# Reordered closing sums of a one-layer decoder kernel, with the norm weights multiplied on GpSimd

## The chip, the cores and the metric

The kernel runs on one core of one Trainium2 chip. The metric is the device time of one execution in microseconds; runs of the kernel before and of the changed kernel are compared by their medians. The engines are named as the profile names them: PE is TensorE, DVE is VectorE, ACT is ScalarE, POOL is GpSimd and SP is SyncE, which only issues transfers here.

## The reference, cut to what matters

One layer of a decoder on 512 tokens of 1024 float32 features: a mixing sub-layer (sparse attention and retention), then a mixture of experts. Only the very end of the second sub-layer is touched here:

```python
def _rms_norm(x, g=None):
    y = xf * lax.rsqrt(jnp.mean(xf * xf, axis=-1, keepdims=True) + EPS)
    return y * g
...
    for e in range(N_EXPERTS):          # 32 experts, each token uses 2 of them
        hid = silu(t @ w_gate_exp[e]) * (t @ w_up_exp[e])
        y = y + combine[:, e:e + 1] * (hid @ w_down_exp[e])
...
    h_res = h_res + gate2 * _rms_norm(ffn, g_post_ffn)
```

So the output is the residual plus a row-normalised sum of two expert rows for each token, times one weight vector (`gate2 * g_post_ffn`, kept in the kernel as `G2`).

## The kernel before

The experts are worked through in units of up to 128 (token, expert) pairs. All units but the last write their weighted rows to `pair_rows` in device memory, two rows for each token (indirect DMAs of GpSimd). The last unit is not written: its 128 rows stay in SBUF (`YO`), and TensorE brings them to their tokens with a product by a 0/1 matrix (`SEL`).

After the last scatter SyncE reads `pair_rows` back in `NB` = 4 blocks of 128 tokens: `YG[b][:, 0, :]` is a token's first row and `YG[b][:, 1, :]` its second (blocks 0 and 1 in the tile `rows`, blocks 2 and 3 in `both_bufs`); semaphore `y_back[b]` tells that block b is there. Then, for each block:

- TensorE (`collect`, L1153 to L1164) writes the 0/1 product to PSUM, two matmuls of 512 columns, each seen in the trace as two records. For blocks 0 and 1 that is all, and DVE adds the two rows of a token itself (`both_rows`, L1957). For blocks 2 and 3 TensorE also adds the second rows, by a product with the identity (L1163), for which it waits on `y_back[b]`.
- DVE adds PSUM to the first rows (`combine`, L1963). This gives the block's sum.
- ACT sums the squares and takes the root (L1407, L1409), DVE inverts it (`invert`, L1967).
- DVE multiplies by `G2` and by the inverse root. For blocks 0 and 1 that is one instruction (`scale`, L1975). For block 2 DVE multiplies by `G2` (`weigh`, L1971) and ACT by the inverse root (L1412). For block 3 DVE does both, and adds the residual in the last step (L1995, in two halves).
- Blocks 0 to 2 go out as accumulating DMAs that GpSimd issues (L2104): the residual already lies in `out`, and the DMA adds to it. Block 3 goes out as two plain halves that SyncE issues (L748).

The order on each engine is the order in which the code is written. A `link` on DVE makes its next instruction wait until the linked one has completed. `y_sum` counts finished sums, `y_scaled` blocks that are ready to go out, and `sel_done` blocks that TensorE has finished.

Of the kernel before, what the change touches and what calls it, by code (L numbers as in the profile page):

```python
# [21 lines left out]
P = 128  # L22
D = 1024
S = 512
NB = S // P
# [237 lines left out]
def build(nc, t, out):  # L263
# [3 lines left out]
    with ExitStack() as ctx:  # L267
# [3 lines left out]
        def sem(name):  # L271
            return ctx.enter_context(nc.semaphore(name))
# [139 lines left out]
        y_sq, o_add = sem("y_sq"), sem("o_add")  # L412
        x2_out, y_inv, y_scaled = sem("x2_out"), sem("y_inv"), sem("y_scaled")
        y_back = [sem(f"y_back{b}") for b in range(NB)]
# [108 lines left out]
        SEL = [score[:, i * S:(i + 1) * S] for i in range(DIRECT)]  # L523
        SUM_BANK, SUMMED = (2, 4, 0, 6), 2

# [230 lines left out]
        def _(pe):  # L756
# [397 lines left out]
            def collect(u, b):  # L1154
                for n in range(2):
                    if b == 0:
                        pe.wait_ge((y_evA, y_evV)[n], NU)
                    c = slice(n * 512, (n + 1) * 512)
                    mm = pe.matmul(ps[SUM_BANK[b] + n][:, :], SEL[u - NS][:, b * P:(b + 1) * P], YO[u % 2][:, c],
                                   start=True, stop=(b < SUMMED))  # L1160
                    if b >= SUMMED:
                        pe.wait_ge(y_back[b], 16)
                        mm = pe.matmul(ps[SUM_BANK[b] + n][:, :], ident, YG[b][:, 1, c], start=False, stop=True)  # L1163
                mm.then_inc(sel_done, 1)  # L1164
# [16 lines left out]
            for b in range(NB):  # L1181
                collect(NS, b)


        @block.scalar
        def _(act):
# [218 lines left out]
            for b in range(NB):  # L1405
                act.wait_ge(y_sum, b + 1)
                a.activation(JUNK2, YG[b][:, 0, :], ACT.Square, accum_out=yss[:, b:b + 1]).then_inc(squared, 1)  # L1407
                act.wait_ge(squared, 2 * NB + b + 1)
                a.activation(yr[:, b:b + 1], yss[:, b:b + 1], ACT.Sqrt, bias=eps, scale=1.0 / D).then_inc(y_sq, 1)  # L1409
                if b == NB - 2:  # L1410
                    act.wait_ge(y_inv, b + 1)
                    a.activation(YG[b][:, 1, :], YG[b][:, 1, :], ACT.Identity, bias=zero,  # L1412
                                 scale=yss[:, b:b + 1]).then_inc(y_scaled, 1)


        @block.vector
        def _(dve):
# [3 lines left out]
            def link(ins):  # L1421

                chained[0] += 1
                ins.then_inc(v_chain, 1)
                dve.wait_ge(v_chain, chained[0])
# [539 lines left out]
            def invert(b):  # L1965
                dve.wait_ge(y_sq, b + 1)
                relay(v.reciprocal(yss[:, b:b + 1], yr[:, b:b + 1]), y_inv, b + 1)  # L1967

            def weigh(b):
                y = YG[b]  # L1970
                link(v.tensor_tensor(y[:, 1, :], y[:, 0, :], G2, ALU.mult))  # L1971

            def scale(b):
                y = YG[b]
                v.scalar_tensor_tensor(out=y[:, 1, :], in0=y[:, 0, :], scalar=yss[:, b:b + 1], in1=G2, op0=ALU.mult,  # L1975
                                       op1=ALU.mult).then_inc(y_scaled, 1)

# [3 lines left out]
            combine(1)  # L1981
            invert(0)
            scale(0)
            combine(2)
            weigh(2)
            invert(1)
            scale(1)
            invert(2)
            combine(3)
            weigh(3)  # L1990
            invert(3)
# [8 lines left out]
        def _(pool):  # L2000
# [98 lines left out]
            each_overflow(pool, lambda: pool.wait_ge(xt_mm, 2 * NU), overflow)  # L2099
            pool.sem_inc(y_base, 1)  # L2100
            pool.wait_ge(x2_out, 16 * NB)
            for b in range(NB - 1):
# [24 lines left out]
```

## Time and profile before

| | us |
|---|---|
| median of 3 runs | 684.8 |
| lowest and highest run | 684.11, 686.64 |
| span of the profiled execution, first to last instruction | 686.0 |

The profiled execution is one more execution. Its own record is the span of 686.0 us, no separate time outside the span is given for it, and the span lies within the three runs. A sum against the trace is therefore a difference against 686.0, and that difference is then put on the median of 684.8.

TensorE is busy for 633.2 us of the span (92%) and DVE for 375.3 us (55%). The stretch that the change touches is the last 23 us, from about 663 us, after the last unit's down projection. In that stretch the shares of the whole span say nothing, and the timeline and the chain of waits are read instead.

### The profile page before, as it was taken

How to read it: one execution, taken by the hardware profiler on the slowest of the kernel's cores; microseconds unless marked ns; L12 is line 12 of the kernel's file. 1: busy time of each engine (PE TensorE's matmuls, PEld its weight loads, DVE VectorE, ACT ScalarE, POOL GpSimd, SP SyncE). 2: the span in 40 equal slices, each digit the busy share in tenths (PEclk: the TensorE clock that was granted, in tenths of full speed). 3: DMA queues.
4: the chain of work that ended last, by engine and by line, in shares of the span. 5: the costliest groups of instructions: out<-in, count | busy, mean ns of one | idle time of the engine just before them, and what ended most of it. 6: DMA issues, size and time to landing. Idle time of an engine off the chain costs nothing.

```text
span 686.0 us, 7088 instructions
## 1 busy us (share of the span) xinstructions
PE 633.2 (92%) x2400; PEld 298.5 (44%) x2400; DVE 375.3 (55%) x721; ACT 206.1 (30%) x411; POOL 100.3 (15%) x96
## 2 busy tenths in 40 slices
PE   1599999999999999999989999989999999988883
PEld 1364444444344444546644556433434453433331
DVE  5765667999786773246863336862323333232055
ACT  1453443334254544431121322111212121221023
POOL 1004333300122221000000000112121211110101
PEclk9999999999999999999989997999999999998998
DMA  9992715240606144070396129799999999999997
GB/s 329 394 374 96 277 28 216 59 187 7 240 0 204 43 147 162 13 241 31 125 383 289 61 86 402 269 370 409 419 421 419 420 419 420 419 418 413 409 411 157
DMA packets 52757, 174.70 MB, mean 255 GB/s; under 512 B 9712, under 2 KB 9712, under 8 KB 41840
## 3 DMA queue, kind: packets, MB, share of 16 engines
q1 hardware_dynamic: 45136, 160.26, 60.3%
q0 software_dynamic: 6160, 12.10, 5.5%
q10 hardware_dynamic: 1424, 1.87, 0.8%
q8 instruction: 20, 0.33, 0.2%
q14 instruction: 17, 0.14, 0.1%
HBM read 168.43 MB, written 15.21 MB: 268 GB/s over the span
## 4 chain that ended last, share of the span: by engine, by line
PE 73%; DVE 11%; DMA 7%; issue 4%; SPq 2%; ACT 1%; POOLq 0%; DVEq 0%; ACTq 0%
PE psum L772 16%; PE psum L1052 15%; PE psum L1113 8%; PE psum L775 8%; PE psum L920 7%; DMA both_bufs<-pair_rows 3%; DMA ring<-in_w_ada 2%; DVE score L1536 2%; PE psum L1025 2%; DVE sm L1535 2%; DVE score L1766 2%; SPq L647 2%; DVE rows L1459 2%; PE psum L877 2%; PE psum L897 1%
## 5 line engine op out<-in xcount | busy, mean ns | idle before, releaser
L772 PE MATMUL psum<-hT,ring 128*128 128x512 f32 (+1 forms) x320 | 135.8, 579 | 0.0
L1052 PE MATMUL psum<-ring,hT 128*64 128x512 f32 (+2 forms) x320 | 92.2, 594 | 1.8 <-DMA ring<-in_w_up_exp 1.4
L772 PEld LDWEIGHTS psum<-hT,ring 128*128 128x128 f32 x320 | 60.2, 192 | 69.4 <-issue 60.1
L775 PE MATMUL psum<-ring,hT 128*128 128x512 f32 x192 | 85.2, 597 | 0.0
L1885 DVE TENSOR_SCALAR work<-work 128x256 f32<-128x256 f32 x16 | 4.6, 290 | 101.8 <-PE psum L1062 76.0
L1248 ACT ACTIVATE both_bufs<-psum 32x512 f32<-32x512 f32 (+2 forms) x68 | 38.3, 563 | 67.7 <-PE psum L772 66.7
L1459 DVE SCALAR_TENSOR_TENSOR rows<-ring,sm,rows 128x512 f32<-128x512 f32 x64 | 55.5, 866 | 1.7
L775 PEld LDWEIGHTS psum<-ring,hT 128*128 128x128 f32 x192 | 35.6, 190 | 44.6 <-issue 44.2
L1052 PEld LDWEIGHTS psum<-ring,hT 128*64 128x64 f32 (+2 forms) x320 | 31.7, 142 | 48.8 <-issue 46.3
L1347 ACT ACTIVATE work<-psum 128x256 f32<-128x256 f32 x17 | 6.5, 383 | 146.7 <-PE psum L1052 146.7
L1113 PE MATMUL psum<-ring,work 128*64 128x512 f32 (+1 forms) x160 | 40.1, 598 | 0.7 <-ACT work L1353 0.7
L2059 POOL DMA_INDIRECT pair_rows<-work,pid_t x16 | 16.0, 1000 | 152.9 <-DVE work L1897 152.9
L1052 PE MATMUL psum<-both_bufs,hT 128*64 128x512 f32 x64 | 31.1, 643 | 3.4 <-issue 3.4
L1052 PE MATMUL psum<-xs,hT 128*64 128x512 f32 x64 | 31.2, 644 | 0.0
L920 PE MATMUL psum<-ring,hT 128*128 128x512 f32 x64 | 30.4, 623 | 0.7 <-ACT hT L1222 0.7
L920 PE MATMUL psum<-ring,work 128*128 128x512 f32 x64 | 28.7, 593 | 0.9 <-ACT work L1301 0.9
L2012 POOL TENSOR_TENSOR both_bufs<-both_bufs 128x512 f32<-128x512 f32 (+1 forms) x13 | 15.5, 1191 | 94.9 <-ACT both_bufs L1248 94.9
L795 PE MATMUL psum<-cst,work 128*64 128x1 f32 x64 | 8.3, 259 | 22.7 <-DVE work L1459 22.7
L1897 DVE TENSOR_SCALAR work<-psum,sinT 128x512 f32<-128x512 f32 x17 | 12.8, 751 | 29.9 <-PE psum L1113 25.4
L1887 DVE RECIPROCAL work<-work 128x256 f32<-128x256 f32 x16 | 28.0, 1753 | 0.5
L1052 PE MATMUL psum<-rows,hT 128*64 128x512 f32 x64 | 28.2, 593 | 0.0
L1535 DVE MAX8 sm<-score 128x8 f32<-128x256 f32 (+2 forms) x48 | 26.7, 556 | 1.2
(322 smaller groups left out, 912.9 us busy)
## 6 DMA issues: line engine op xcount, KB each, us to landing
ring<-in_w_down_exp SPq DMA_DIRECT2D x20, 1024.0 KB, 18.4
ring<-in_w_in SPq DMA_DIRECT2D x8, 2048.0 KB, 9.3
ring<-in_w_ada SPq DMA_DIRECT2D x8, 2048.0 KB, 13.8
ring<-in_w_gate_exp SPq DMA_DIRECT2D x14, 1024.0 KB, 20.2
ring<-in_w_up_exp SPq DMA_DIRECT2D x14, 1024.0 KB, 23.0
ring<-in_w_ada SPq DMA_DIRECT2D x7, 1024.0 KB, 13.3
ring<-in_w_gate_exp SPq DMA_DIRECT2D x12, 512.0 KB, 15.2
ring<-in_w_up_exp SPq DMA_DIRECT2D x12, 512.0 KB, 15.4
```

What stands on the lines that cost most here:

```text
L647: sp.dma_start(chunk(n)[:, lo:hi, :], w_ada[:, lo:hi, what * 512:(what + 1) * 512]).then_inc(signal, 16)
L772: mm = pe.matmul(o[:, at], w[:, k, b * P:(b + 1) * P], hT3[:, k, at], start=(k == 0), stop=(k == KD - 1))
L775: mm = pe.matmul(o[:, :], hT3[:, k, b * P:(b + 1) * P], w[:, k, :], start=(k == 0), stop=(k == KD - 1))
L920: mm = pe.matmul(o[:, :], mixed, w[:, k, :], start=(k == 0), stop=(k == KD - 1))
L1052: mm = pe.matmul(o[rows, :], XT[u % 2][:, k, rows], both(GU_SLOT[place])[:, k, :, :], start=(k == 0), stop=(k == KD - 1))
L1113: mm = pe.matmul(o[rows, :], HT[u % 2][:, i, rows], down_of(DOWN_SLOT[place])[:, i, n * 512:(n + 1) * 512], start=(i == 0), stop=(i == KF ...
L1248: ins = a.activation(SWAPPED[r % 2][here, at], bank(s)[there, at], ACT.Copy)
L1459: ins = v.scalar_tensor_tensor(out=acc, in0=w[:, k, :], scalar=sc_[:, k:k + 1], in1=acc, op0=ALU.mult, op1=ALU.add)
L1535: link(v.max(top8, m))
L1887: v.reciprocal(e, e).then_inc(gu_step, 1)
L2012: g.tensor_tensor(other, other, trig[table][:, 1, at], ALU.mult).then_inc(crossed, 1)
L2059: g.indirect_dma_start(out=y_dram, out_offset=bass.IndirectOffsetOnAxis(ap=pid_t[:, u:u + 1], axis=0), in_=YO[u % 2], in_offset=None, boun ...
```

## The change

- TensorE does the 0/1 products of all four blocks first, without waiting for a transfer, and signals each block as its product is ready. It adds second rows for block 3 alone, behind all products (`add_last_rows`). Block 2's rows are now added by DVE (`both_rows(2)`).
- GpSimd multiplies the sums of blocks 0, 1 and 2 by `G2`. Its DMA issues stand behind all three multiplications in its program.
- DVE's `scale` is now a multiplication by the inverse root alone (one tensor and one scalar of each partition), and waits for GpSimd's product.
- ACT no longer scales block 2.
- DVE's order is new: the sums of blocks 2 and 3 stand ahead of the scaling of block 1.

```diff
@@ TensorE
                 for n in range(2):
                     if b == 0:
                         pe.wait_ge((y_evA, y_evV)[n], NU)
-                    c = slice(n * 512, (n + 1) * 512)
-                    mm = pe.matmul(ps[SUM_BANK[b] + n][:, :], SEL[u - NS][:, b * P:(b + 1) * P], YO[u % 2][:, c],
-                                   start=True, stop=(b < SUMMED))
-                    if b >= SUMMED:
-                        pe.wait_ge(y_back[b], 16)
-                        mm = pe.matmul(ps[SUM_BANK[b] + n][:, :], ident, YG[b][:, 1, c], start=False, stop=True)
+                    mm = pe.matmul(ps[SUM_BANK[b] + n][:, :], SEL[u - NS][:, b * P:(b + 1) * P],
+                                   YO[u % 2][:, n * 512:(n + 1) * 512], start=True, stop=(b < NB - 1))
+                if b < NB - 1:
+                    mm.then_inc(sel_done, 1)
+
+            def add_last_rows():
+
+                b = NB - 1
+                pe.wait_ge(y_back[b], 16)
+                for n in range(2):
+                    mm = pe.matmul(ps[SUM_BANK[b] + n][:, :], ident, YG[b][:, 1, n * 512:(n + 1) * 512], start=False,
+                                   stop=True)
                 mm.then_inc(sel_done, 1)
@@ ScalarE
                 a.activation(yr[:, b:b + 1], yss[:, b:b + 1], ACT.Sqrt, bias=eps, scale=1.0 / D).then_inc(y_sq, 1)
-                if b == NB - 2:
-                    act.wait_ge(y_inv, b + 1)
-                    a.activation(YG[b][:, 1, :], YG[b][:, 1, :], ACT.Identity, bias=zero,
-                                 scale=yss[:, b:b + 1]).then_inc(y_scaled, 1)
@@ VectorE
-            def weigh(b):
-                y = YG[b]
-                link(v.tensor_tensor(y[:, 1, :], y[:, 0, :], G2, ALU.mult))
-
             def scale(b):
                 y = YG[b]
-                v.scalar_tensor_tensor(out=y[:, 1, :], in0=y[:, 0, :], scalar=yss[:, b:b + 1], in1=G2, op0=ALU.mult,
-                                       op1=ALU.mult).then_inc(y_scaled, 1)
+                dve.wait_ge(y_weighed, b + 1)
+                v.tensor_scalar(y[:, 1, :], y[:, 1, :], yss[:, b:b + 1], None, ALU.mult).then_inc(y_scaled, 1)
 
             both_rows(0)
             combine(0)
             both_rows(1)
             combine(1)
             invert(0)
+            both_rows(2)
             scale(0)
             combine(2)
-            weigh(2)
             invert(1)
+            combine(3)
             scale(1)
+            link(v.tensor_tensor(YG[3][:, 1, :], YG[3][:, 0, :], G2, ALU.mult))
             invert(2)
-            combine(3)
-            weigh(3)
+            scale(2)
             invert(3)
@@ GpSimd
             pool.sem_inc(y_base, 1)
+            for b in range(NB - 1):
+                pool.wait_ge(y_sum, b + 1)
+                g.tensor_tensor(YG[b][:, 1, :], YG[b][:, 0, :], G2, ALU.mult).then_inc(y_weighed, 1)
             pool.wait_ge(x2_out, 16 * NB)
             for b in range(NB - 1):
                 pool.wait_ge(y_scaled, b + 1)
```

The order on DVE before, from the second `both_rows` (L1957) to the last reciprocal (`rows` holds blocks 0 and 1, `both_bufs` blocks 2 and 3, `work` in an operand is `G2`):

```order
L1957 TENSOR_TENSOR rows<-rows 128x1024 [waits y_back1,y_sum]
L1963 TENSOR_TENSOR rows<-rows,psum 128x1024 [waits sel_done,v_chain]
L1967 RECIPROCAL sm<-sm 128x1 [waits y_sq,y_sum]
L1975 SCALAR_TENSOR_TENSOR rows<-rows,sm,work 128x1024 [waits y_inv]
L1963 TENSOR_TENSOR both_bufs<-both_bufs,psum 128x1024 [waits sel_done]
L1971 TENSOR_TENSOR both_bufs<-both_bufs,work 128x1024 [waits y_sum]
L1967 RECIPROCAL sm<-sm 128x1 [waits y_sq,v_chain]
L1975 SCALAR_TENSOR_TENSOR rows<-rows,sm,work 128x1024 [waits y_inv]
L1967 RECIPROCAL sm<-sm 128x1 [waits y_sq]
L1963 TENSOR_TENSOR both_bufs<-both_bufs,psum 128x1024 [waits sel_done,y_inv]
L1971 TENSOR_TENSOR both_bufs<-both_bufs,work 128x1024 [waits y_sum]
L1967 RECIPROCAL sm<-sm 128x1 [waits y_sq,v_chain]
```

Each sum of blocks 2 and 3 is followed directly by its product with `G2`. The same stretch of DVE after the change, from the first reciprocal on:

```order
L1970 RECIPROCAL sm<-sm 128x1 [waits y_sq,y_sum]
L1960 TENSOR_TENSOR both_bufs<-both_bufs 128x1024 [waits y_back2,y_inv]
L1975 TENSOR_SCALAR rows<-rows,sm 128x1024 [waits y_weighed,v_chain]
L1966 TENSOR_TENSOR both_bufs<-both_bufs,psum 128x1024 [waits sel_done]
L1970 RECIPROCAL sm<-sm 128x1 [waits y_sq,y_sum]
L1966 TENSOR_TENSOR both_bufs<-both_bufs,psum 128x1024 [waits sel_done,y_inv]
L1975 TENSOR_SCALAR rows<-rows,sm 128x1024 [waits y_weighed,y_sum]
L1988 TENSOR_TENSOR both_bufs<-both_bufs,work 128x1024
L1970 RECIPROCAL sm<-sm 128x1 [waits y_sq,v_chain]
L1975 TENSOR_SCALAR both_bufs<-both_bufs,sm 128x1024 [waits y_weighed,y_inv]
L1970 RECIPROCAL sm<-sm 128x1 [waits y_sq]
```

The second-row sum of block 2 (L1960) has come in ahead of the first scaling, and the first scaling waits both for it (`v_chain`) and for GpSimd (`y_weighed`). On GpSimd, the end of the program, the difference of after against before:

```order
-L2104 DMA out<-rows 128x1024 [waits y_scaled,x2_out]
-L2104 DMA out<-rows 128x1024 [waits y_scaled]
-L2104 DMA out<-both_bufs 128x1024 [waits y_scaled]
+L2103 TENSOR_TENSOR rows<-rows,work 128x1024 [waits y_sum] x2
+L2103 TENSOR_TENSOR both_bufs<-both_bufs,work 128x1024 [waits y_sum]
+L2107 DMA out<-rows 128x1024 [waits y_scaled,x2_out]
+L2107 DMA out<-rows 128x1024 [waits y_scaled]
+L2107 DMA out<-both_bufs 128x1024 [waits y_scaled]
```

The three issues of the accumulating DMAs have moved behind three multiplications, the last of which waits for the third sum.

## Rows read from the trace of the kernel before

**Rows 1.** Chain that ended last, in order of time: start us, us, what.

```profile
649.90 18.68 DMA both_bufs<-pair_rows
...
668.62 1.12 PE psum L1163 x2
...
675.61 1.24 ACT both_bufs L1412
...
678.64 0.75 DVE both_bufs L1995
```

**Rows 2.** Timeline: start us, us, engine, line, operation, out<-in, shape, count, idle before.

```profile
663.32 4.53 PE L1159 MATMUL psum<-work,score 128*128 128x512 f32 x10
...
666.63 1.23 DVE L1957 TENSOR_TENSOR rows<-rows 128x1024 f32<-128x1024 f32 x1
...
667.89 1.22 DVE L1963 TENSOR_TENSOR rows<-rows,psum 128x1024 f32<-128x1024 f32 x1
...
669.35 1.28 DVE L1975 SCALAR_TENSOR_TENSOR rows<-rows,sm,work 128x1024 f32<-128x1024 f32 x1
...
671.23 0.99 POOL L2104 DMA_DIRECT2D out<-rows  x1 [30.00 <-DVE rows L1975]
...
675.80 0.89 POOL L2104 DMA_DIRECT2D out<-rows  x1 [3.59 <-DVE rows L1975]
...
677.14 0.84 POOL L2104 DMA_DIRECT2D out<-both_bufs  x1 [0.45 <-ACT both_bufs L1412]
...
679.42 1.23 SPq L748 DMA_DIRECT2D out<-both_bufs  x2
```

**Rows 3.** Windows: stretch, length, busy of each engine, PEclk, DMA share, GB/s.

```profile
672.40:676.00 3.60, 2.50 (x6) 0.76 (x4) 3.46 (x6) 1.84 (x4) 0.20 (x1) 1.00 0.90 146
676.00:677.20 1.20, 0.00 (x0) 0.00 (x0) 1.17 (x2) 1.19 (x2) 0.75 (x2) 1.00 0.01 0
677.20:680.40 3.20, 0.00 (x0) 0.00 (x0) 2.46 (x4) 1.11 (x3) 0.78 (x1) 0.87 1.11 170
680.40:683.20 2.80, 0.00 (x0) 0.00 (x0) 0.00 (x0) 0.00 (x0) 0.00 (x0) 0.50 0.97 195
683.20:684.80 1.60, 0.00 (x0) 0.00 (x0) 0.00 (x0) 0.00 (x0) 0.00 (x0) 0.50 0.79 302
```

**Rows 4.** Instructions of the tile `pair_rows` from 600 us on, transfer times.

```profile
DMA to landing us min/median/max: 6.7/11.8/20.7
```

**Rows 5.** Timeline: POOL's products of two float32 SBUF tensors, early in the kernel.

```profile
64.78 1.00 POOL L2012 TENSOR_TENSOR both_bufs<-both_bufs 128x384 f32<-128x384 f32 x1 [2.76 <-ACT both_bufs L1248]
...
94.04 1.27 POOL L2012 TENSOR_TENSOR both_bufs<-both_bufs 128x512 f32<-128x512 f32 x1 [5.08 <-ACT both_bufs L1248]
```

**Rows 6.** Timeline: three places where DVE and POOL work at once.

```profile
79.48 1.34 POOL L2012 TENSOR_TENSOR both_bufs<-both_bufs 128x512 f32<-128x512 f32 x1 [3.89 <-ACT both_bufs L1248]
79.73 1.37 DVE L1481 TENSOR_SCALAR xs<-xs 128x512 f32<-128x512 f32 x1
...
86.29 0.69 DVE L1521 TENSOR_TENSOR work<-psum,both_bufs 128x512 f32<-128x512 f32 x1 [2.03 <-ACT both_bufs L1248]
86.35 1.27 POOL L2012 TENSOR_TENSOR both_bufs<-both_bufs 128x512 f32<-128x512 f32 x1 [2.63 <-ACT both_bufs L1248]
86.90 0.86 DVE L1764 TENSOR_SCALAR score<-both_bufs,sm 128x256 f32<-128x256 f32 x1
...
196.41 3.21 DVE L1459 SCALAR_TENSOR_TENSOR rows<-ring,sm,rows 128x512 f32<-128x512 f32 x3
196.53 1.75 POOL L2015 TENSOR_TENSOR ring<-ring,both_bufs 128x512 f32<-128x512 f32 x1
```

**Rows 7.** Groups by line and shape: count, busy us, mean ns, idle before.

```profile
L1481 DVE TENSOR_SCALAR both_bufs<-both_bufs 128x512 f32<-128x512 f32 x1 | 0.4, 426 | 0.0
...
L1764 DVE TENSOR_SCALAR score<-both_bufs,sm 128x512 f32<-128x512 f32 x1 | 0.5, 486 | 0.0
L1764 DVE TENSOR_SCALAR score<-both_bufs,sm 128x384 f32<-128x384 f32 x1 | 0.4, 408 | 0.0
```

More of the change, by code:

```diff
@@ L412, in build @@
         y_sq, o_add = sem("y_sq"), sem("o_add")
-        x2_out, y_inv, y_scaled = sem("x2_out"), sem("y_inv"), sem("y_scaled")
+        x2_out, y_inv, y_scaled, y_weighed = sem("x2_out"), sem("y_inv"), sem("y_scaled"), sem("y_weighed")
         y_back = [sem(f"y_back{b}") for b in range(NB)]
@@ L523, in build @@
         SEL = [score[:, i * S:(i + 1) * S] for i in range(DIRECT)]
-        SUM_BANK, SUMMED = (2, 4, 0, 6), 2
+        SUM_BANK = (2, 4, 0, 6)
         def load_gate(sp, e, s, signal):
@@ L1182, in _ @@
                 collect(NS, b)
+            add_last_rows()
         @block.scalar
```

## The prediction

> **What bounds the kernel now.** The change touches only the end, so I read the chain that ended last first, then the timeline from 663 us, then the windows of the DMA engines there. The chain [rows 1] shows that the end hangs on the read-back of block 2: that transfer lands at 668.58, TensorE adds its second rows from 668.62, DVE and ACT finish blocks 2 and 3, and DVE's last two halves start at 678.64. SyncE issues the last two transfers at 679.42 [rows 2].
>
> What the chain does not show is how full the DMA engines are behind that. GpSimd issues the accumulating transfers of blocks 0, 1 and 2 at 671.23, 675.80 and 677.14 [rows 2]. The first has the engines to itself: from 672.40 to 676.00 they move 3.6 x 146 = 526 KB, one block, at a share of 0.90. Then they idle (676.00 to 677.20, share 0.01). From 677.20 to 683.20 the share is about 1 and 3.2 x 170 + 2.8 x 195 = 1090 KB pass, which is blocks 1 and 2. The last block follows until 684.80 (1.6 x 302 = 483 KB), and the span ends at 686.0 [rows 3]. So a block by an accumulating transfer costs the engines 2.8 to 3.6 us, a plain one some 1.4 us, and from 677.2 to the end this is a queue that never runs dry. Block 0's transfer is out of that queue only because it starts 4.6 us earlier than the second. **The end is a matter of when the accumulating transfers can start, as much as of the last sum.**
>
> **The change part by part.**
>
> TensorE. The eight 0/1 products need 16 records. Ten took 4.53 us from 663.32 [rows 2], so at 0.43 each all 16 end at about 670.3. Block 3's second rows come with the slowest read-back: issued at about 650.4, landing after 20.7 us [rows 4], at 671.1. Two more matmuls (four records, 1.8 us) make block 3's product ready at about 672.9, where before DVE could begin that sum only at 675.61. Taken alone this is a gain of up to 2.7 us. Block 2 needs no matmul after its landing any more.
>
> GpSimd, the price of one multiplication. Its products of two SBUF tensors take 1.00 us for 384 columns and 1.27 for 512 [rows 5], so 0.27 for each 128 more, and 2.36 us for 1024 columns (an estimate along that line). Two instructions of 512 columns would take 2.54, which bounds it from above, and DVE's 1.23 for such a pair of tensors [rows 2] from below; the line through the two rows of the same operation is nearest. DVE did block 0's whole scaling in 1.28 us [rows 2].
>
> DVE and GpSimd at the same time. This is the term that decides. At 79.48 GpSimd starts a product of 1.34 us and DVE a one-tensor multiplication at 79.73 [rows 6], which alone takes 0.426 [rows 7]. It takes 1.37 and ends at 81.10, 0.28 after GpSimd's end at 80.82: it waited for the whole of GpSimd's instruction. With the scalar taken from SBUF, which is the form of the new `scale`, it is the same: 0.86 us for 256 columns at 86.90, ending 0.14 after GpSimd [rows 6], where 0.33 would be expected from 0.408 and 0.486 for 384 and 512 columns [rows 7]. DVE's addition that reads PSUM, at 86.29 beside the same GpSimd product, took its plain 0.69. The other way round, at 196.41 DVE starts the first of three additions of two SBUF tensors, and GpSimd's product at 196.53 takes 1.75 instead of 1.27, while DVE's three take 3.21 together [rows 6], about 1.0 more than three of the 0.75 that L1995, of the same kind and size, takes [rows 1]: GpSimd waited for DVE's first, and DVE's second for all of GpSimd. It follows that `both_rows`, the new `scale` and DVE's product with `G2` take turns with GpSimd's multiplications in whole instructions, and `combine` (which reads PSUM) does not. At a handover about 0.15 us is saved.
>
> The Trainium skill (SBUF — State Buffer, section SBUF: two separate sides) calls this an exclusive lock on a port pair, held for the full instruction, and names two-input and fast-mode DVE instructions; by it the term would be the same, and the trace agrees with 1.37 us against 0.43.
>
> Now the walk. Until 667.86 nothing moves: `both_rows(1)` starts at 666.63, as soon as the first sum is done and before GpSimd can, and ends at 667.86 [rows 2].
> - GpSimd's block 0: 667.86 + 2.36 - 0.15 = 670.1. Beside it DVE does `combine(1)` and the reciprocal.
> - `both_rows(2)` (data there since 668.58) waits, then 670.1 + 1.23 - 0.15 = 671.2.
> - GpSimd's block 1 is ready since 669.1. DVE's next instruction waits for `both_rows(2)` to complete (`v_chain`), and into that gap GpSimd steps, as it did at 197: 671.2 + 2.2 = 673.4.
> - `scale(0)` is held until then. Its own price is 0.486 + 4 x 0.078 = 0.80 [rows 7], so it ends at 674.0.
> - `combine(2)` stands behind it on DVE: 674.05 to 675.3. Before, it ended at 672.7.
> - GpSimd's block 2 waits for that: 675.4 to 677.8. DVE's reciprocal and `combine(3)` pass beside it, until 676.7, but `scale(1)` waits for 677.8 and ends at 678.4.
> - The product of block 3 with `G2` ends at 679.7, the reciprocal at 679.9, `scale(2)` at 680.7, the last reciprocal at 680.9. The last halves start at 680.9, and SyncE issues at about 681.7 and 682.4.
>
> TensorE's gain is thus not used: block 3's product waits from 672.9 to 675.5 for DVE. ACT's removed 1.24 us [rows 1] is no loss and no gain, since its squares are ready long before.
>
> GpSimd's DMA issues stand behind its third multiplication: the first goes out at 677.85 instead of 671.23, although block 0 is scaled at 674.0. The second follows at about 678.8 and the third at about 681.1. From issue to data it was 1.2 us for the first before (671.23 to 672.4), so the engines start at 679.05. They have three accumulating blocks and one plain one: 6.0 for two of them as before, 2.7 to 3.5 for the third, 1.4 for the last block, and 1.4 from the last data to the end of the span (684.6 to 686.0). 679.05 + 6.0 + 2.7 + 1.4 + 1.4 = 690.55, which is **4.6 us over 686.0**; with 3.5 it is 5.4. If all three flow at 2.7, it is 3.9. I take 4.6, since the third comes out of a queue that is already running, as the second of before did. The DVE side alone would end later by 681.7 - 679.4 = 2.3 us, so the queue of transfers decides.
>
> Put on the median: 684.8 + 4.6 = 689.4.
>
> **The rivals.**
>
> GpSimd does not get its turn between `both_rows(2)` and `scale(0)`. Against it speaks the wait for completion between the two; for it, that no row shows a DVE instruction this short behind. Then `scale(0)` ends at 672.0, `combine(2)` at 673.3, GpSimd's multiplications at 674.4 and 676.8, and all is 1.0 us earlier: +3.6, 688.4.
>
> The instructions do not hinder each other at this size. Then `combine(2)` ends at 672.5, the third multiplication at 675.0, and the first transfer is issued at 675.1. The queue of three still costs: 675.1 + 1.2 + 8.7 + 2.8 = 687.8 to 688.6, so +1.8 to +2.6, 686.6 to 687.4. Rows 6 speak against it.
>
> Not slower: the accumulating transfers are bound by their own latency and run side by side when all three wait at once. It decides if, with three queued, the bytes per us rise clearly over 195 GB/s. With hardly any hindrance on DVE, the last halves start at 677.1, 1.5 us before 678.64, and the result is 683.3. Against it: two transfers already overlapped in 677.2 to 683.2, and the rate was 170 to 195, not twice 146 [rows 3].
>
> Worse: the DMA descriptors of GpSimd are held up as its arithmetic is. `scale(1)` runs from 677.8 as the first issue starts, which would add up to 0.65 us; with the dear third transfer, 4.6 + 0.8 + 0.65 = +6.1, 690.9. The product with `G2` at 676.86 did not lengthen the issue at 677.14 (0.84 against 0.99 and 0.89) [rows 2].
>
> For this last point the Trainium skill (SBUF — State Buffer, the box on DVE blocking DMA) says that a fast-mode DVE instruction keeps GpSimd from writing descriptors. No run here shows it with `scale`'s form.
>
> **How the numbers follow.** The forecast 0.56, GpSimd's missed turn 0.14, no hindrance 0.16, transfers side by side 0.06, worse 0.08. Half a per cent is about what a measurement of this kernel can tell from no change, 3.4 us, so the border is 688.2. The forecast and the worse case lie above it almost wholly (0.54 and 0.07), of the missed turn a little over half (0.08): slower 0.69. The rest is same, 0.28, with 0.03 left for faster. The range goes from the lower end of no hindrance, 686.6, to the worse case, 691.0, and leaves out the side-by-side case and some of the worse.
>
> **What would show it.** In the profile after: GpSimd's three multiplications at about 667.9, 671.2 and 675.4 and each 2.2 to 2.5 us of own work; `scale(0)` ending right after the second of them, with 2.2 us of waiting inside it; `combine(2)` ending near 675.3; GpSimd's first DMA at 677.9; a DMA share near 1 without a hole from 679 to 689; the idle hole of before at 676.00 to 677.20 grown to the whole stretch from about 672.5 to 679. The prediction is wrong if `scale(0)` and `both_rows(2)` take 0.8 and 1.2 us beside GpSimd's work, or if three queued transfers take clearly less than 8 us.

## The result, and the profile after

The changed kernel takes 690.77 us in the median of four runs (689.47 to 692.2), against 685.07 us of four runs of the kernel before (684.11 to 686.64). The ratio is 1.0086, with a 95% interval of 1.0062 to 1.0110. It is slower by 5.7 us; forecast were 4.6 us and 689.4 us, in a range of 686.6 to 691.0 us. Among the runs further below, one execution of 1653.61 us (the kernel before with block 1 scaled early) is left out of the ratio.

The profiled execution of after has a span of 687.6 us, only 1.6 more than the 686.0 of before. That is no contradiction: the stretch ahead of the change differs from execution to execution by several us (TensorE's first 0/1 product starts at 663.32 in before and at 659.71 in after). All that the change does comes behind that product, so two profiles are compared here mainly by the **tail**: from the start of the first 0/1 product to the end of the span. It is 686.0 - 663.32 = 22.7 us before and 687.6 - 659.71 = 27.9 us after, 5.2 us more.

The timeline of after, in the columns of [rows 2] (L1960 adds second rows, L1966 is `combine`, L1975 `scale`, L1988 the product of block 3 with `G2`, L2103 GpSimd's multiplication, L2107 its DMA issues):

```profile
659.71 7.10 PE L1158 MATMUL psum<-work,score 128*128 128x512 f32 x16
...
663.03 1.23 DVE L1960 TENSOR_TENSOR rows<-rows 128x1024 f32<-128x1024 f32 x1
663.08 6.68 POOL L2103 TENSOR_TENSOR rows<-rows,work 128x1024 f32<-128x1024 f32 x2 [25.72 <-DVE rows L1966]
...
665.74 1.82 DVE L1960 TENSOR_TENSOR both_bufs<-both_bufs 128x1024 f32<-128x1024 f32 x1
...
667.56 1.98 PE L1168 MATMUL psum<-both_bufs,cst 128*128 128x512 f32 x4 [0.75 <-DMA both_bufs<-pair_rows]
667.59 2.72 DVE L1975 TENSOR_SCALAR rows<-rows,sm 128x1024 f32<-128x1024 f32 x1
670.23 1.21 DVE L1966 TENSOR_TENSOR both_bufs<-both_bufs,psum 128x1024 f32<-128x1024 f32 x1
...
671.52 2.36 POOL L2103 TENSOR_TENSOR both_bufs<-both_bufs,work 128x1024 f32<-128x1024 f32 x1 [1.76 <-DVE both_bufs L1966]
671.67 1.22 DVE L1966 TENSOR_TENSOR both_bufs<-both_bufs,psum 128x1024 f32<-128x1024 f32 x1
...
672.93 1.50 DVE L1975 TENSOR_SCALAR rows<-rows,sm 128x1024 f32<-128x1024 f32 x1
673.83 1.93 POOL L2107 DMA_DIRECT2D out<-rows  x2
...
675.80 0.75 DVE L1975 TENSOR_SCALAR both_bufs<-both_bufs,sm 128x1024 f32<-128x1024 f32 x1
...
676.66 1.42 DVE L1995 SCALAR_TENSOR_TENSOR both_bufs<-both_bufs,sm,xs 128x512 f32<-128x512 f32 x2
676.85 0.84 POOL L2107 DMA_DIRECT2D out<-both_bufs  x1 [1.10 <-DVE both_bufs L1975]
677.44 1.00 SPq L748 DMA_DIRECT2D out<-both_bufs  x2
```

Three things are to be seen. The same DVE instruction L1975 takes 2.72, 1.50 and 0.75 us: 0.75 is its own price, the rest is time in which GpSimd works (until 669.76 and 673.88). GpSimd's first two multiplications take 6.68 us together, where the third, undisturbed, takes 2.36. And GpSimd's first transfer is issued at 673.83, 14.1 us behind the first product, against 7.9 in before.

The windows of after, in the columns of [rows 3], show what the transfers make of it:

```profile
673.00:675.20 2.20, 0.00 (x0) 0.00 (x0) 2.20 (x2) 1.37 (x3) 2.20 (x3) 0.50 0.00 0
675.20:678.00 2.80, 0.00 (x0) 0.00 (x0) 2.69 (x6) 0.00 (x0) 1.40 (x2) 0.50 1.01 142
678.00:681.00 3.00, 0.00 (x0) 0.00 (x0) 0.08 (x1) 0.00 (x0) 0.00 (x0) 0.50 1.07 197
681.00:684.00 3.00, 0.00 (x0) 0.00 (x0) 0.00 (x0) 0.00 (x0) 0.00 (x0) 0.50 1.03 230
684.00:685.80 1.80, 0.00 (x0) 0.00 (x0) 0.00 (x0) 0.00 (x0) 0.00 (x0) 0.50 0.74 233
685.80:687.60 1.80, 0.00 (x0) 0.00 (x0) 0.00 (x0) 0.00 (x0) 0.00 (x0) 0.50 0.00 0
```

The DMA engines stand still until 675.2 and are then full until the last data at about 685.6: all four blocks pass in one run of 10.4 us, in which no engine of the core computes after 678.1. In before the first block had passed ahead of that run.

### The profile page after: what moved, and what is told of

Read it like the earlier page. It is cut to its first block, busy times and chain, and to the rows that moved or that the text cites. A ratio compares the mean times of both kernels' runs of the same rounds, so it can differ in the third digit from the quotient of the medians.

```text
span 687.6 us, 7087 instructions
## 1 busy us (share of the span) xinstructions
PE 627.4 (91%) x2396; PEld 295.7 (43%) x2396; DVE 378.2 (55%) x722; ACT 205.0 (30%) x410; POOL 109.5 (16%) x99
## 4 chain that ended last, share of the span: by engine, by line
PE 70%; DVE 13%; DMA 7%; issue 5%; SPq 3%; ACT 1%; DVEq 0%; POOLq 0%; ACTq 0%
PE psum L772 16%; PE psum L1052 15%; PE psum L1113 8%; PE psum L775 8%; PE psum L920 7%; DMA ring<-in_w_ada 2%; DMA ring<-in_w_down_exp 2%; DVE score L1539 2%; PE psum L1025 2%; DVE sm L1538 2%; DMA work<-h_rows,tok_t 2%; DVE score L1769 2%; SPq L647 2%; DVE rows L1462 2%; PE psum L897 2%
## 5 line engine op out<-in xcount | busy, mean ns | idle before, releaser
L775 PE MATMUL psum<-ring,hT 128*128 128x512 f32 x192 | 85.2, 596 | 0.0
L2012 POOL TENSOR_TENSOR both_bufs<-both_bufs 128x512 f32<-128x512 f32 (+1 forms) x13 | 15.5, 1192 | 96.2 <-ACT both_bufs L1255 96.2
L920 PE MATMUL psum<-ring,hT 128*128 128x512 f32 x64 | 28.7, 594 | 0.7 <-ACT hT L1229 0.7
```

Of the source, the lines that this page charges most:

```text
L775: mm = pe.matmul(o[:, :], hT3[:, k, b * P:(b + 1) * P], w[:, k, :], start=(k == 0), stop=(k == KD - 1))
L920: mm = pe.matmul(o[:, :], mixed, w[:, k, :], start=(k == 0), stop=(k == KD - 1))
L2012: g.tensor_tensor(other, other, trig[table][:, 1, at], ALU.mult).then_inc(crossed, 1)
```

## The experiments

Tails are read from one profiled execution each, medians and ratios from the timed runs beside the kernel before on the same chip. Two executions of the same kernel differed in the tail by 0.4 us (before) and by 1.7 us (after), so a single tail is good for differences of some 2 us, not of 0.5. A table first:

| kernel | first product, span | tail | first transfer issued, behind the first product |
|---|---|---|---|
| before | 663.32, 686.0 | 22.7 | 7.9 |
| before, a second execution | 659.91, 683.0 | 23.1 | 7.9 |
| after | 659.71, 687.6 | 27.9 | 14.1 |
| after, a second execution | 661.28, 690.9 | 29.6 | 15.9 |
| after, block 0's transfer issued early | 658.61, 684.8 | 26.2 | 10.9 |
| after, no multiplication on GpSimd | 659.95, 683.8 | 23.9 | 9.2 |
| after, multiplications in halves | 664.55, 694.1 | 29.5 | 14.5 |
| the same, a second execution | 661.37, 689.9 | 28.5 | 13.3 |
| after, plain transfers | 658.41, 681.5 | 23.1 | 14.1 |
| after, last halves held | 657.60, 686.2 | 28.6 | 14.1 |
| after, GpSimd first at block 0 | 657.51, 687.8 | 30.3 | 16.1 |
| before, issues held | 661.14, 689.6 | 28.5 | 14.1 |
| before, block 1 scaled early | 658.59, 679.4 | 20.8 | 7.9 |
| the same, 0/1 products first | 659.10, 680.2 | 21.1 | 7.9 |

**Is it the issue order on GpSimd?**

```diff
-            for b in range(NB - 1):
+            def weigh(b):
                 pool.wait_ge(y_sum, b + 1)
                 g.tensor_tensor(YG[b][:, 1, :], YG[b][:, 0, :], G2, ALU.mult).then_inc(y_weighed, 1)
-            pool.wait_ge(x2_out, 16 * NB)
-            for b in range(NB - 1):
+
+            def send(b):
                 pool.wait_ge(y_scaled, b + 1)
                 pool.dma_start(out_blocks[b], YG[b][:, 1, :], accum_op=ALU.add).then_inc(y_both[b], 16)
+
+            pool.wait_ge(x2_out, 16 * NB)
+            weigh(0)
+            weigh(1)
+            send(0)
+            weigh(2)
+            send(1)
+            send(2)
```

The wait for `x2_out` now stands ahead of the multiplications too. It costs nothing here: the first of them starts 3.44 us behind the first product, 3.37 in after.

> The changed kernel, with GpSimd issuing block 0's accumulating transfer between its second and third multiplication instead of behind all three. Measured on the tail, from TensorE's first 0/1 product to the end of the span: 22.7 us before, 27.9 after. If the queue of accumulating transfers sets the end (theory), this one leaves at about 670.5 instead of 673.8 on the clock of the profile after and fills a stretch in which the DMA engines are idle; the other two leave as in after, so the tail shrinks by 2.0 to 3.3 us, to 24.6 to 25.9. If DVE's later finish sets the end (rival), DVE's chain is unchanged and the tail stays at 27.5 to 28.

Measured: median 687.56 us, ratio 1.0030 (0.9996 to 1.0063), tail 26.2. Its windows:

```profile
670.60:674.20 3.60, 0.00 (x0) 0.00 (x0) 3.56 (x3) 2.64 (x6) 2.73 (x2) 0.56 0.91 145
674.20:674.80 0.60, 0.00 (x0) 0.00 (x0) 0.56 (x2) 0.00 (x0) 0.50 (x1) 0.50 0.06 7
674.80:682.60 7.80, 0.00 (x0) 0.00 (x0) 2.26 (x5) 0.00 (x0) 0.84 (x1) 0.50 0.97 201
```

Block 0 passes ahead of the others again (3.6 x 145 = 522 KB). The tail shrinks by 1.7 us, less than the 2.0 expected at the least. In windows of 0.1 us block 1's data start at 675.2, 16.6 us behind the first product. Its run with block 2 and the last block takes 7.5 us (before needed 7.4 for the same), and 2.1 us follow behind the last data where before had 1.4. The median is 2.3 us over that of before, where after lay 5.7 us over it. DVE's chain ends no earlier than in after (its last halves start 17.1 behind the first product, 16.95 in after), so the rival, an end set by DVE, falls.

**Is it GpSimd's arithmetic?**

```diff
-                dve.wait_ge(y_weighed, b + 1)
-                v.tensor_scalar(y[:, 1, :], y[:, 1, :], yss[:, b:b + 1], None, ALU.mult).then_inc(y_scaled, 1)
+                v.scalar_tensor_tensor(out=y[:, 1, :], in0=y[:, 0, :], scalar=yss[:, b:b + 1], in1=G2, op0=ALU.mult,
+                                       op1=ALU.mult).then_inc(y_scaled, 1)
...
-            for b in range(NB - 1):
-                pool.wait_ge(y_sum, b + 1)
-                g.tensor_tensor(YG[b][:, 1, :], YG[b][:, 0, :], G2, ALU.mult).then_inc(y_weighed, 1)
```

> The changed kernel without GpSimd's multiplications: DVE multiplies by both factors in one instruction, as before, in the new order. If whole-instruction hindrance between DVE and GpSimd is the cost (theory), the second rows of block 2 take 1.22 us, combine(2) ends about 1.9 us earlier than in after (9.8 us behind the first 0/1 product instead of 11.7), block 0's transfer leaves 5 us earlier, and the tail is 22.7 to 24. If the new order of DVE and TensorE were itself the cost (rival), the tail stays above 26.

Measured: median 685.24 us, ratio 1.0001 (0.9964 to 1.0037), tail 23.9. From its timeline:

```profile
665.98 1.23 DVE L1960 TENSOR_TENSOR both_bufs<-both_bufs 128x1024 f32<-128x1024 f32 x1
...
667.25 1.28 DVE L1974 SCALAR_TENSOR_TENSOR rows<-rows,sm,work 128x1024 f32<-128x1024 f32 x1
...
668.45 1.21 DVE L1966 TENSOR_TENSOR both_bufs<-both_bufs,psum 128x1024 f32<-128x1024 f32 x1
```

`both_rows(2)` takes 1.23 instead of 1.82 us, and `combine(2)` starts 8.5 us behind the first product instead of 10.5. More work for DVE is less time for it: scaling with both factors costs 1.28 us, the "cheaper" form cost 2.72. The new order of TensorE and DVE without GpSimd's part is no gain either: blocks 0 and 2 leave at 9.2 and 15.5 us instead of 7.9 and 13.8, and the tail is 1.2 us over the first of before's and 0.8 over the second. The timed runs show no difference from before.

By the tails the two experiments split the 5.2 us into 1.7 for the issue order (27.9 to 26.2), 2.3 for GpSimd's arithmetic (26.2 to 23.9) and 1.2 for the rest of the reordering (23.9 to 22.7). By the medians over before they split 5.7 us into 3.4, 2.3 and nothing (5.7, 2.3, 0.0). Each of the two ratios is uncertain by about 0.35%, or 2.4 us. Both ways give 2.3 us for GpSimd's arithmetic, and its timeline shows the waits that are gone; that the issue order costs more than 1.7 us, and the rest of the reordering less than 1.2, is likely by the medians but not settled.

**One whole instruction, or shared bandwidth?**

```diff
-                dve.wait_ge(y_weighed, b + 1)
+                dve.wait_ge(y_weighed, 2 * b + 2)
...
-                g.tensor_tensor(YG[b][:, 1, :], YG[b][:, 0, :], G2, ALU.mult).then_inc(y_weighed, 1)
+                for c in HALVES:
+                    g.tensor_tensor(YG[b][:, 1, c], YG[b][:, 0, c], G2[:, c], ALU.mult).then_inc(y_weighed, 1)
```

> The changed kernel with each of GpSimd's multiplications cut into two instructions of 512 columns. If the loser waits for one whole instruction (theory), DVE's waits beside GpSimd shrink from 0.6 and 1.9 us to at most 1.3 each, both engines alternate at the cut, and scale(0) ends earlier than 10.6 us behind the first product, by up to 1 us, or GpSimd's second product ends later by a DVE instruction. If the bandwidth were shared instead (rival), the sums of the times would not change by the cut and scale(0) ends where it did, within 0.2 us. The tail moves by less than 1.5 us either way.

Measured: median 691.05 us, ratio 1.0062 (1.0040 to 1.0084). In the profiled execution the read-back of block 2 landed 6.9 and that of block 3 9.3 us behind the first product, instead of 5.3 and 7.8. So the end of `scale(0)` (10.9 instead of 10.6) says nothing about the cut into halves, and the tail of 29.5, 1.7 us over that of after where less than 1.5 was expected, says little. It was run once more:

> Once more the kernel with GpSimd's multiplications in halves, since in its first execution the read-back of blocks 2 and 3 landed 1 to 1.5 us later than elsewhere. With the read-back at its usual place (5.3 and 7.8 us), no wait of DVE for GpSimd is longer than 1.27 us, where the longest in after was 1.97. The tail is 27.5 to 28.5 by the theory, since the same work passes the same port.

Measured: 691.72 us in one run, tail 28.5 (661.37 to 689.9). The timeline, with the read-back in its place:

```profile
664.74 7.42 POOL L2104 TENSOR_TENSOR rows<-rows,work 128x512 f32<-128x512 f32 x4 [25.44 <-DVE rows L1966]
...
667.40 1.96 DVE L1960 TENSOR_TENSOR both_bufs<-both_bufs 128x1024 f32<-128x1024 f32 x1
...
669.40 1.64 DVE L1975 TENSOR_SCALAR rows<-rows,sm 128x1024 f32<-128x1024 f32 x1
```

The first scaling takes 1.64 us, 0.9 over its own 0.75, where it had waited 1.97 in after; the longest wait is now 0.9, less than the 1.25 us of one half (the third product's two halves take 2.50). It ends 9.7 us behind the first product instead of 10.6. GpSimd finishes its two products at 10.8 instead of 10.05, since DVE has come in between. So the loser waits for one instruction, and the length of that instruction bounds its wait. The tail did not follow (28.5 against 27.9 or 29.6), though the first transfer left 0.8 us earlier than in after (13.3). The windows at the end show where it was lost:

```profile
686.37:687.37 1.00, 0.00 (x0) 0.00 (x0) 0.00 (x0) 0.00 (x0) 0.00 (x0) 0.50 0.09 25
687.37:688.37 1.00, 0.00 (x0) 0.00 (x0) 0.00 (x0) 0.00 (x0) 0.00 (x0) 0.50 0.03 12
688.37:689.37 1.00, 0.00 (x0) 0.00 (x0) 0.00 (x0) 0.00 (x0) 0.00 (x0) 0.50 0.00 0
```

The bulk of the data has passed at 686.4, 25.0 us behind the first product, against about 25.9 in after: that part did follow. But 1.6 us more pass at a share of 0.07 (until 688.0), about one of the 16 engines, where after has less than 0.5 us of this. The first execution in halves ends the same way (0.08 from 690.6 to 692.2). What holds these last packets back is open, and nothing shows that it has to do with the halves: by the medians, 691.05 against 690.77, they changed nothing that can be told.

**Do the accumulating transfers set the end?**

```diff
-                pool.dma_start(out_blocks[b], YG[b][:, 1, :], accum_op=ALU.add).then_inc(y_both[b], 16)
+                pool.dma_start(out_blocks[b], YG[b][:, 1, :]).then_inc(y_both[b], 16)
```

> The changed kernel with plain instead of accumulating transfers for blocks 0 to 2: it leaves out the addition of the residual for them, so its output is not the reference's. If the accumulating transfers' time on the DMA engines sets the end (theory), each of the three costs about 1.3 us instead of 2.7 to 3.5, the engines are free when the last block comes, which then lands about 3 us after its issue, and the tail shrinks by 3.5 to 5 us, to 23 to 24.4. If it is DVE's chain (rival), the tail shrinks by less than 1.5 us.

Measured: median 685.06 us, ratio 0.9991 (0.9962 to 1.0020), tail 23.1. Its transfers (out<-in, queue, count, KB each, us from issue to landing):

```profile
out<-rows POOLq DMA_DIRECT2D x2, 512.0 KB, 3.4
...
out<-both_bufs POOLq DMA_DIRECT2D x1, 512.0 KB, 3.7
...
out<-both_bufs SPq DMA_DIRECT2D x2, 256.0 KB, 3.2
```

And the window in which all four blocks pass:

```profile
673.70:679.50 5.80, 0.00 (x0) 0.00 (x0) 2.96 (x6) 0.00 (x0) 0.83 (x2) 0.50 0.92 361
```

All arithmetic is as slow as in after (the last halves start 16.95 us behind the first product), and yet no loss is left that the timed runs or the tail show. The four blocks need 5.8 us instead of 10.4. The 1.6 us by which DVE ends later than in before are hidden under the transfers in after.

**The queue alone.** The kernel before, with nothing changed in any engine's arithmetic:

```diff
-                pool.wait_ge(y_scaled, b + 1)
+                pool.wait_ge(y_scaled, NB - 1)
```

> The kernel before, with one edit: GpSimd's three issues all wait until block 2 is scaled. No engine's arithmetic changes. If the queue sets the end (theory), the three leave at 13.8, 14.8 and 15.7 us behind the first 0/1 product instead of 7.9, 12.5 and 13.8, the DMA engines need 8.7 us for them from 15.1 on and 2.8 for the rest, and the tail grows from 22.7 to 26 to 27.2. If three queued transfers run side by side (rival), it grows by less than 1 us.

Measured: median 691.8 us, ratio 1.0085 (1.0056 to 1.0115), tail 28.5. Holding the transfers of blocks 0 and 1 back costs 5.8 us of tail, as much as the whole change, and 6.7 us of median. Its windows:

```profile
676.30:686.60 10.30, 0.00 (x0) 0.00 (x0) 1.54 (x3) 0.00 (x0) 1.76 (x2) 0.58 0.99 202
686.60:689.60 3.00, 0.00 (x0) 0.00 (x0) 0.00 (x0) 0.00 (x0) 0.00 (x0) 0.50 0.01 4
```

The queue of three accumulating blocks and a plain one takes 10.3 us, as worked out (8.7 + 1.4 = 10.1). Three at once do not run side by side. In windows of 0.1 us it runs from 676.7 to 687.0, so each border of the windows above lies some 0.4 us early. The tail is 1.3 us over the 27.2 expected at the most, and the largest part of that stands behind the last data: 2.6 us until the end of the span, where it was 1.4 in before.

**What lies behind the last data.** That stretch is 1.4 us in before, 1.9 in after, 2.1 in the kernel with the early issue and 2.6 with the issues held, in windows of 0.1 us; the coarser windows above give 2.0, 2.2 and 3.0. My theory was that plain halves issued right behind the last accumulating transfer mix with it.

```diff
+            sp.wait_ge(y_both[0], 16)
             for part, c in enumerate(HALVES):
                 sp.wait_ge(o_add, part + 1)
```

> The changed kernel, where SyncE issues the last block's two plain halves only when block 0's accumulating transfer has landed, about 19.6 us behind the first 0/1 product instead of 17.7. In after the halves were issued 0.6 us behind GpSimd's last issue, in the kernel before 2.3 us behind it, and the time from the last data to the end of the span was 2.1 against 1.4. If the mixing of plain and accumulating transfers costs the 0.6 us by which the forecast was short (theory), the tail shrinks from 27.9 to 26.8 to 27.4 although a transfer starts later. If it does not (rival), the tail is 27.8 or longer.

Measured: median 690.13 us, ratio 1.0063 (1.0036 to 1.0090), tail 28.6 (657.60 to 686.2). The halves left at 19.8 us. The window behind the bulk of the data:

```profile
683.90:686.20 2.30, 0.00 (x0) 0.00 (x0) 0.00 (x0) 0.00 (x0) 0.00 (x0) 0.50 0.04 16
```

A few packets pass in it until 684.6, and the 1.6 us behind them are hardly shorter than the 1.9 of after. The tail is not shorter either: DVE and GpSimd run as in after to 0.02 us, yet it is 0.7 us longer, with data until 27.0 us behind the first product instead of 26.0, perhaps because the halves themselves left 2.1 us later. The theory finds no support. What makes the last landing later is open.

**How far executions differ.**

> The kernel before unchanged, for the same purpose: tail within 0.5 us of 22.7.

> The changed kernel unchanged, to see how far two executions differ in the stretch behind the first 0/1 product. If the tail is a property of the order of the work, it repeats within 0.5 us of 27.9, whatever the span does ahead of it.

Measured: before again 23.1, within the bound. After again 29.6, 1.7 us longer, which my expectation excluded. Its timeline shows a different order:

```profile
664.66 2.35 POOL L2103 TENSOR_TENSOR rows<-rows,work 128x1024 f32<-128x1024 f32 x1 [26.98 <-DVE rows L1966]
...
665.22 2.86 DVE L1960 TENSOR_TENSOR rows<-rows 128x1024 f32<-128x1024 f32 x1 [0.65 <-DMA rows<-pair_rows]
...
669.42 2.35 POOL L2103 TENSOR_TENSOR rows<-rows,work 128x1024 f32<-128x1024 f32 x1 [2.42 <-DVE rows L1966]
...
669.57 3.28 DVE L1960 TENSOR_TENSOR both_bufs<-both_bufs 128x1024 f32<-128x1024 f32 x1
```

The read-back of block 1 landed 0.65 us behind the first sum. In the first profile of after DVE went first at this place by 0.05 us (663.03 against 663.08); here GpSimd did, and `both_rows(1)`, which everything behind it waits for, took 2.86 us. `both_rows(2)` then met the whole of the second multiplication and took 3.28. To see whether the order does that, or the late landing:

```diff
             combine(0)
+            dve.wait_ge(y_weighed, 1)
             both_rows(1)
```

> The changed kernel, where DVE adds the second rows of block 1 only when GpSimd has multiplied block 0, so that GpSimd always goes first. In the second execution of after the read-back of block 1 landed 0.6 us behind the first sum, GpSimd took the port first, and the tail was 29.6 instead of 27.9 us. If who comes first at this place is what tells the two apart (theory), the tail is 29.4 to 30.0 with the read-back at its usual place, block 0's transfer leaves at 15.7 to 16.1 instead of 14.1, and the median is 1 to 2 us over that of after. If the late read-back did it by itself (rival), the tail stays within 0.6 us of 27.9.

Measured: median 692.81 us, ratio 1.0120 (1.0078 to 1.0162), tail 687.8 - 657.51 = 30.3. From its timeline:

```profile
660.88 2.34 POOL L2104 TENSOR_TENSOR rows<-rows,work 128x1024 f32<-128x1024 f32 x1 [28.68 <-DVE rows L1966]
...
663.31 1.23 DVE L1960 TENSOR_TENSOR rows<-rows 128x1024 f32<-128x1024 f32 x1 [2.52 <-POOL rows L2104]
...
673.60 1.93 POOL L2108 DMA_DIRECT2D out<-rows  x2
```

The first transfer left at 16.1 us, as expected, the tail is 0.3 us over the range, and the median is 2.0 us over that of after. Here DVE waits by the program and not for the port, but the order and the delay are those of the longer execution. GpSimd's going first is enough for the longer tail, and it needs no late landing. The four timed runs of after fall into 689.47 and 689.50 against 692.05 and 692.20. A half of them with the one order and a half with the other would look like that. But the stretch ahead of the tail varies by more than this (the first product starts at 663.32 and at 659.91 us in the two profiles of before), and only two executions of after have a trace, so for the four it is a guess.

**Can the hole be used?** If the transfers set the end, then the kernel before gains by moving a transfer forward, not by shortening a sum. Block 1's scaling fits into the 0.9 us in which DVE waited for TensorE:

```diff
             scale(0)
+            invert(1)
+            scale(1)
             combine(2)
             weigh(2)
-            invert(1)
-            scale(1)
             invert(2)
```

> The kernel before, with block 1's inversion and scaling moved ahead of the sum of block 2 on DVE, into the 0.9 us in which DVE waits for TensorE. If the queue of transfers sets the end (theory), block 1's transfer leaves about 3 us earlier, right behind block 0's, the idle 1.2 us of the DMA engines goes, and the tail shrinks by 1 to 2 us, to 20.7 to 21.7. If DVE's last step sets it (rival), it moves by at most 0.5 us, since the last halves start at most 0.5 us earlier.

Measured: median 683.32 us in all twelve runs, 682.86 without the one of 1653.61 us, against 685.08, ratio 0.9977 (0.9955 to 0.9999), tail 20.8. From its timeline:

```profile
666.12 1.28 DVE L1975 SCALAR_TENSOR_TENSOR rows<-rows,sm,work 128x1024 f32<-128x1024 f32 x1
666.50 0.99 POOL L2104 DMA_DIRECT2D out<-rows  x1 [31.00 <-DVE rows L1975]
...
667.71 0.89 POOL L2104 DMA_DIRECT2D out<-rows  x1 [0.22 <-issue]
...
671.89 0.84 POOL L2104 DMA_DIRECT2D out<-both_bufs  x1 [3.29 <-ACT both_bufs L1412]
...
674.16 1.00 SPq L748 DMA_DIRECT2D out<-both_bufs  x2
```

And its window from the first data to the last:

```profile
667.70:677.90 10.20, 2.46 (x6) 0.76 (x4) 6.25 (x8) 4.13 (x7) 1.73 (x2) 0.80 1.00 205
```

The second issue follows the first at once, the DMA engines are full for about 10 us without a hole, and the tail is 1.9 us shorter although DVE's last halves start only 0.5 us earlier. By the ratio this version is 1.6 us faster than before, with an interval from 0.1 to 3.1 us: it ends just under 1, so a small gain is likely and its size is not well known. Against after it is clear.

> As the run with block 1's scaling first, and TensorE does all 0/1 products ahead of the second rows of blocks 2 and 3. By the theory the sum of block 2 can start 1 us earlier and that of block 3 2 us earlier, but the queue of transfers takes it up again: tail within 0.7 us of the one without this edit, 20 to 21.7. If a sum still set the end (rival), the tail shrinks by another 1 us or more.

The edit, on top of the last one: the 0/1 products of all blocks first, then the second rows of blocks 2 and 3.

```diff
...
+            def add_rows(b):
+                pe.wait_ge(y_back[b], 16)
+                for n in range(2):
+                    mm = pe.matmul(ps[SUM_BANK[b] + n][:, :], ident, YG[b][:, 1, n * 512:(n + 1) * 512], start=False,
+                                   stop=True)
                 mm.then_inc(sel_done, 1)
...
             for b in range(NB):
                 collect(NS, b)
+            for b in range(SUMMED, NB):
+                add_rows(b)
```

Measured: median 683.77 us, ratio 0.9981 (0.9959 to 1.0004), tail 680.2 - 659.10 = 21.1. TensorE's part of the change, in this kernel, brings nothing. But the run does not show that the queue takes an earlier sum up, since no sum came earlier: `combine(2)` starts 8.86 us behind the first product instead of 8.74, and `combine(3)` 11.89 instead of 11.76, because DVE is busy ahead of both or waits for ACT. The 1 and 2 us that I expected there were not to be had.

## Why the prediction was right

**The hindrance in whole instructions** held at every step up to GpSimd's first issue, to 0.4 us. On the clock of after (3.61 us ahead of before's) the walk had `both_rows(2)` ending at 671.2 - 3.6 = 667.6 (measured 667.56), `scale(0)` at 670.4 (670.31), `combine(2)` at 671.7 (671.44), the third multiplication at 674.2 (673.88) and GpSimd's first issue at 674.24 (673.83). The multiplication was put at 2.36 us from the rows for 384 and 512 columns [rows 5] and took 2.36. The new `scale` was put at 0.80 [rows 7] and took 0.75. DVE's last halves were put at 677.3 and started at 676.66; with the DMA engines busy until 685.6 that 0.6 us did not count. The rival of a missed turn did not occur: GpSimd stepped into the gap before `scale(0)`. The rule of the Trainium skill that the prediction named (SBUF — State Buffer, SBUF: two separate sides), an exclusive lock for a full instruction, agrees with the 2.72 against 0.75 us and with the shorter wait when GpSimd's instruction was halved; and `combine(3)`, which reads PSUM, took its plain 1.22 beside GpSimd, as that page's exception has it.

**The queue of transfers** was the term that set the end, as said. The run of data was put at 10.1 us and took 10.4, and the run with the issues held, without any hindrance, had 10.3.

**The side-by-side rival** and the one without hindrance are excluded by the held issues and by after's own rows. For the worse case, held-up DMA descriptors, there is no sign: the first two issues took 1.93 us together, beside `scale(1)`, against 0.99 + 0.89 in [rows 2], and the first data came 1.4 us behind the issue. In windows of 0.1 us that is 1.4 in before too (672.6, behind 671.23): the 1.2 us of the prediction is the border of a window that was drawn 0.2 us early.

**Two terms were mis-sized.** The time behind the last data was taken as 1.4 from before and was 2.0 in after. With the 0.3 us of the queue, and less the 0.2 us by which the first data came earlier than in the walk (15.5 instead of 15.7 us behind the first product: the issue 0.4 earlier, its data 0.2 later), that makes the 5.2 instead of 4.6 in this profile. And the sentence that `both_rows(1)` starts before GpSimd can was true by 0.05 us only. I had read it as settled, and gave it no rival. It depends on the landing of a transfer, and where it goes the other way the tail is 29.6 instead of 27.9. That is the step to be marked as weak, and possibly part of the way from the forecast of 689.4 to the median of 690.8. That the median lies in the range at all, 0.2 us below its end of 691.0, owes something to luck: two of the four runs, 692.05 and 692.20, lie outside.

**TensorE's part** brought block 3's product early and unused, as said: it was complete at 669.5 in after and read at 671.67.

## What to carry to other kernels

Before work is moved from DVE to GpSimd, look for the places in the trace where both work at once: two-input and one-tensor SBUF instructions of DVE and arithmetic of GpSimd take turns here, so the sum of both engines' times is what counts, and a wait of 0.05 us decides which goes first. Where the last stage writes to memory, read the share of the DMA engines behind the last sum: if it is full, a step is worth what it moves the start of the transfers or how much of a hole between them it closes, not what it saves on the chain, and an issue must not stand behind other work in its queue. A hole between transfers is the place to look for a gain.

## What the runs showed of the hardware that I had not expected

An accumulating transfer of 512 KB from SBUF occupies the DMA engines for about 3.4 us alone (672.6 to 676.0 in before) and for about 3.0 us in a queue of three, a plain one for about 1.4 (5.8 us for four blocks in a row, 10.3 to 10.4 with three of them accumulating). From GpSimd's issue to the first data it is 1.4 us in before and in after alike. The time from the last data to the end of the span is not a constant: 1.4 us in before, 1.9 in after, 2.6 where all accumulating transfers were issued together. And the last packets can trail behind the bulk, on about one of the 16 engines, for 1.6 us in one execution and for less than 0.5 us in another.
